# A two-block transformer on one core: loads, panel splits and squares moved to other places in their queues

## The chip, the cores and the metric

The kernel runs on one core of a Trainium2 chip. The metric is device time in microseconds of one execution of the whole program, the median of several runs. Five engines work from instruction queues of their own: TensorE (PE), VectorE (DVE), ScalarE (ACT), GpSimd (POOL) and SyncE (SP), which here issues the large loads. They meet at semaphores.

## The reference

256 tokens of width 1024 go through two models one behind the other, all in float32.

```python
def reference(x, ...):
    x = first_block(x, ...)      # 2 layers: x += hybrid_mixer(rms_norm(x)); x += conv_ffn(rms_norm(x))
    return second_block(x, ...)  # 2 layers: h += 0.5 * rms_norm(swiglu(rms_norm(h)))
                                 #           h += rms_norm(mixer(rms_norm(h)))
                                 #           h += 0.5 * rms_norm(swiglu(rms_norm(h)))
def conv_ffn(h, w_up, conv_w, conv_b, w_down):
    a, g = jnp.split(h @ w_up, 2, axis=-1)
    a = causal_depthwise_conv(a, conv_w) + conv_b          # 3 taps
    return (jax.nn.gelu(a) * g) @ w_down
def swiglu(x, w_gate_up, w_down):
    gate, up = jnp.split(x @ w_gate_up, 2, axis=-1)
    return (jax.nn.silu(gate) * up) @ w_down
```

The hybrid mixer is three kinds of attention with gated branches; the second block's mixers are a short convolution and a gated delta rule (the "delta" stage), whose heads' outputs are normalized: `o * rsqrt(mean(o * o) + eps) * norm_w * silu(z)`, and then multiplied by `w_out`.

## The kernel before

**Stages.** Ten stages in a row: HYBRID, FFN1, HYBRID, FFN1, then FFN2, SHORT, FFN2, FFN2, DELTA, FFN2. Each begins with `turn_x` on TensorE (transposes of x by the identity in `masks`), `prepare` on ACT and `prepare_tile` on DVE, which bring x with its gain into `xhi` and `xlo`, and a root of the row sums. FFN1, FFN2, SHORT and HYBRID then run `blocks_of`, blocks of 128 hidden features: 22 in FFN1 and FFN2, 8 in HYBRID and SHORT. DELTA runs `delta`, 47 slots in an order written out by hand, and then 16 blocks.

**Precision.** Every product of activations and weights is made of three matmuls, hi x hi, lo x hi and hi x lo. A weight panel (128 x 1024, 512 KB) lands in `raw[p % 6]`; ACT copies it into `whi` (`hi(p)`, L988), DVE subtracts and gets `wlo` (`lo(p)`, L1516), and TensorE waits for `lo_done`. The 621 panels form one stream through a ring of six. SP loads panel p once `lo` of panel p-6 is done; `hi(p)` also waits until TensorE has used panel p-6. The stream's order on ACT and DVE is the order in which the code calls `hi_to` and `lo_to`.

**A block** f of an FFN stage: TensorE multiplies two up panels (48 matmuls of 256 columns) and then the down panel of block f-2 (12 matmuls of 512 columns, L2275 to L2277 like the others). DVE scales the up products (`gate_scaled`), ACT applies the tap (L1046) and Gelu (FFN1) or Silu (FFN2), DVE multiplies to h, ACT copies h into `hhi` (L1059), and DVE makes `hlo` from it in block f+1 (`h_low`, L1676). In HYBRID the up product is one panel, and DVE gates three branches (L1617 to L1624). In DELTA's blocks TensorE transposes two tiles of a head's output (L2371) and multiplies the down panel of block f-2; DVE makes h from the transposes (L1667).

**Around the delta stage's end** ACT squares the last set's outputs (`delta_o_squared`, eight squares, L1415) in the last slot, DVE sums them (`delta_o_added`, L2181), ACT takes the root behind block 1, and DVE scales the last two pairs behind block 2.

**The start.** SP issues x, cols, masks and six panels. ACT waits for cols, calls `hi_to(1)` (panels 0 and 1), then `prepare(0)`. DVE calls `lo_to(1)` and then makes the eight `xlo` tiles. TensorE waits for masks and x. GpSimd waits for masks and then issues the small loads of the hybrid stage (w1, w2, pos, gate_w among them, which DVE waits for in tile 1, L1799).

Of the kernel before, what the change touches and what calls it, by code (L numbers as in the profile page):

```python
# [300 lines left out]
def build(nc, stages, arrays):  # L301
# [14 lines left out]
    with ExitStack() as ctx:  # L316
# [459 lines left out]
        def _(sp):  # L776
            sp.dma_start(x[:], x_in).then_inc(x_loaded, 16)
            sp.dma_start(cols[:], cols_in).then_inc(cols_loaded, 16)
            sp.dma_start(masks[:], masks_in).then_inc(masks_loaded, 16)
# [81 lines left out]
        def _(pool):  # L861
# [4 lines left out]
            pool.wait_ge(masks_loaded, 16)  # L866
            def hybrid(s):
# [110 lines left out]
        def _(act):  # L978
# [16 lines left out]
            def prepare(s):  # L995

                for k in range(KT):
                    g, src = turned(s, k)
                    if k == TURNS[g][0]:
                        act.wait_ge(x_turned, len(TURNS) * s + g + 1)  # L1000
                    act.activation(xhi[:, k, :], src, ACT.Copy, scale=col(("pre", s), k)).then_inc(xhi_ready, 1)  # L1001
                if posts_before(s):
                    act.wait_ge(post_squared, QUARTERS * posts_before(s))
# [28 lines left out]
            def ffn_block(s, f, turn):  # L1032
# [7 lines left out]
                elif kind in (FFN2, DELTA):  # L1040
                    act.activation(act_out[:, sl, :], first[:, sl, 2:], ACT.Silu).then_inc(act_done, 1)  # L1041
                elif kind != HYBRID:

                    c = plus(convs_before(s) + f, turn, UNROLL)
                    if kind == FFN1:
                        act.activation(conv[:, sl, :], first[:, sl, 2:], ACT.Identity,  # L1046
                                       scale=tap(s, 2, f, turn), bias=conv_bias(s, f, turn)) \
                            .then_inc(tap_done, 1)
                        act.wait_ge(conv_done, c + 1)
# [9 lines left out]
                act.activation(hhi[:, sl, :], h[:, sl, :], ACT.Copy).then_inc(hhi_done, 1)  # L1059

            def blocks_of(s):
                def body(f, turn):
                    nb = n_blocks(s)
                    if turn is not None:
                        for j in range(n_up(s) + 1):
                            hi(up_panel(s, f + 1, j), turn)
                        split[0] = up_panel(s, nb - 2, n_up(s)) + 1
                    else:
                        hi_to(ahead_panel(s, f + 1 if stages[s][0] == HYBRID and 0 < f < nb - 1 else f))
                    ffn_block(s, f, turn)  # L1070
                    if f == 1 and stages[s][0] == DELTA:
                        delta_o_root(1)
                    if f == nb - 1:
                        hi_to(down_panel(s, f) + LEAD)
                run_blocks(act, s, body)
# [332 lines left out]
            def delta_o_squared(n):  # L1408

                act.wait_ge(d["o_copied"], 2 * (n + 1))  # L1410
                for i in range(SET * CHUNKS):
# [13 lines left out]
            def delta_step(s, n, o):  # L1425
# [17 lines left out]
                if p == 22:  # L1443
                    delta_o_squared(n)
# [40 lines left out]

            act.wait_ge(cols_loaded, 16)
            act.wait_ge(consts_ready, 4)
            hi_to(1)
# [13 lines left out]
        def _(dve):  # L1502
# [95 lines left out]
            def ffn_block(s, f, turn):  # L1598
# [13 lines left out]
                elif kind == HYBRID:  # L1612

                    dve.wait_ge(y["merged"], 3 * KT * (hybrids_before(s) + 1))
# [10 lines left out]
                    if f >= 1:  # L1625
                        h_low(s, f - 1, turn)
# [13 lines left out]
                else:  # L1640
                    dve.tensor_tensor(first[:, sl, 2:], pair[:, 0:S], rstd[:], ALU.mult).then_inc(gate_scaled, 1)  # L1641
                    dve.tensor_tensor(second[:, sl, :], pair[:, S:], rstd[:], ALU.mult).then_inc(pair_read, 1)

# [35 lines left out]
            def blocks_of(s):  # L1679
                def body(f, turn):  # L1680
                    nb = n_blocks(s)
                    if turn is not None:
                        for j in range(n_up(s) + 1):
                            lo(up_panel(s, f + 1, j), turn)
                        split[0] = up_panel(s, nb - 2, n_up(s)) + 1
                    else:
                        lo_to(ahead_panel(s, f))
                    ffn_block(s, f, turn)
                    if f == 2 and stages[s][0] == DELTA:
                        delta_o_inv(1)  # L1690
                        delta_o_scaled((6, 7))
# [510 lines left out]
            def delta_step(s, n, o):  # L2202
# [23 lines left out]
                if p == (23 if n + 1 < SETS else 22):  # L2226
                    delta_o_added(n)
# [29 lines left out]
            dve.wait_ge(consts_ready, 4)  # L2257
            lo_to(1)
            for k in range(KT):
                prepare_tile(0, k)  # L2260
# [11 lines left out]
        def _(pe):  # L2272
# [650 lines left out]
            pe.wait_ge(consts_ready, 4)  # L2923
            pe.wait_ge(masks_loaded, 16)
# [24 lines left out]
```

## Time and profile before

| | |
|---|---|
| runs, median (lowest to highest) | 2023.91 us (2023.28 to 2025.52), 3 runs |
| profiled execution: time, span | 2025.12 us, 2023.3 us |
| TensorE busy (matmuls / weight loads) | 1979.2 us, 98% / 1841.5 us, 91% |
| DVE, ACT, GpSimd busy | 1389.5 us, 69% / 1105.3 us, 55% / 125.4 us, 6% |
| mean granted clock of TensorE | 0.995 |
| mean DMA rate | 172 GB/s |

The span runs from the first to the last instruction of the profiled execution; the time of an execution is a little longer. Busy shares are means over stages with different limits. The granted clock is a share of 2.4 GHz: TensorE runs either at that or at half of it.

### The profile page before, as it was taken

To read this page: it belongs to the slowest core of one execution; us is meant where nothing else is said; L and a number is where in the kernel's file an instruction comes from. 1 tells how busy PE (TensorE), PEld (TensorE's weight loads), DVE (VectorE), ACT (ScalarE), POOL (GpSimd) and SP (SyncE) were. 2 spreads that over 40 slices of the span, in tenths; PEclk is the share of its full clock that TensorE was granted. 3 is DMA by queue.
4 is the path that set the end of the run, shared out by engine and by line. 5 is a ranking of instruction groups with operands and counts; after the bars stand their busy time and mean duration, and the time that the engine had idled before them with its cause. 6 is when DMAs were issued, how large, how long until landed. Compare 5 with 4: busy or idle time off the path is not lost. (4 is left out here: it accounts for less than half of the span.)

```text
span 2023.3 us, 40582 instructions
## 1 busy us (share of the span) xinstructions
PE 1979.2 (98%) x15118; PEld 1841.5 (91%) x15118; DVE 1389.5 (69%) x2352; ACT 1105.3 (55%) x1836; POOL 125.4 (6%) x204
## 2 busy tenths in 40 slices
PE   8999999999999999999999999999999999999998
PEld 6999899989998999899999999999999999979997
DVE  5687877676788777765567765575559876567555
ACT  5665555566654655554454544464448786546443
POOL 2031000000130000000000000000002422000000
PEclk9999999999999999999999999999999999999999
DMA  9433655554335555465546455555555444345552
GB/s 309 146 126 126 210 193 187 191 178 146 133 119 177 178 187 187 167 208 187 188 166 212 154 195 187 187 178 187 188 178 166 134 140 149 126 146 186 187 188 93
DMA packets 117812, 348.42 MB, mean 172 GB/s; under 512 B 23288, under 2 KB 35912, under 8 KB 117184
## 3 DMA queue, kind: packets, MB, share of 16 engines
q1 hardware_dynamic: 114960, 335.23, 48.9%
q0 software_dynamic: 2736, 11.59, 1.8%
q8 instruction: 80, 1.31, 0.3%
q14 instruction: 36, 0.29, 0.0%
HBM read 340.81 MB, written 5.96 MB: 171 GB/s over the span
## 5 line engine op out<-in xcount | busy, mean ns | idle before, releaser
L1516 DVE TENSOR_TENSOR wlo<-raw,whi 128x1024 fp32r<-128x1024 f32 x621 | 737.9, 1229 | 382.6 <-ACT whi L988 381.5
L2275 PE MATMUL bank<-xhi,whi 128*128 128x256 f32 x3368 | 955.5, 284 | 9.7 <-DVE xlo L1527 5.2
L2276 PE MATMUL bank<-xlo,whi 128*128 128x256 f32 x3368 | 941.7, 280 | 0.0
L2277 PE MATMUL bank<-xhi,wlo 128*128 128x256 f32 x3368 | 941.1, 279 | 0.0
L2275 PEld LDWEIGHTS bank<-xhi,whi 128*128 128x128 f32 x3368 | 633.8, 188 | 25.2 <-issue 7.3
L2276 PEld LDWEIGHTS bank<-xlo,whi 128*128 128x128 f32 x3368 | 634.2, 188 | 5.7
L2277 PEld LDWEIGHTS bank<-xhi,wlo 128*128 128x128 f32 x3368 | 633.6, 188 | 0.0
L988 ACT ACTIVATE whi<-raw 128x1024 fp32r<-128x1024 f32 x621 | 621.2, 1047 | 6.8 <-PE bank L2277 5.3
L2275 PE MATMUL bank<-whi,hhi 128*128 128x512 f32 x688 | 273.7, 398 | 6.5 <-DVE hlo L1676 5.1
L2277 PE MATMUL bank<-whi,hlo 128*128 128x512 f32 x688 | 271.6, 395 | 0.0
L2276 PE MATMUL bank<-wlo,hhi 128*128 128x512 f32 x688 | 271.1, 394 | 0.0
L1059 ACT ACTIVATE hhi<-h 128x256 fp32r<-128x256 f32 x172 | 72.1, 419 | 266.7 <-PE bank L2277 182.6
L1041 ACT ACTIVATE act_out<-first 128x256 f32<-128x256 f32 x89 | 37.4, 420 | 230.7 <-DVE first L1641 230.3
L2275 PEld LDWEIGHTS bank<-whi,hhi 128*128 128x128 f32 x688 | 129.5, 188 | 34.8 <-issue 10.5
L2277 PEld LDWEIGHTS bank<-whi,hlo 128*128 128x128 f32 x688 | 129.8, 189 | 30.2
L2276 PEld LDWEIGHTS bank<-wlo,hhi 128*128 128x128 f32 x688 | 130.4, 190 | 23.3
L1641 DVE TENSOR_TENSOR first<-bank,rstd 128x256 f32<-128x256 f32 x132 | 55.8, 422 | 52.8 <-PE bank L2277 52.6
L1676 DVE TENSOR_TENSOR hlo<-h,hhi 128x256 fp32r<-128x256 f32 x172 | 71.8, 417 | 12.6 <-ACT hhi L1059 12.6
L1046 ACT ACTIVATE conv<-first,cols 128x256 f32<-128x256 f32 x44 | 26.5, 603 | 92.9 <-DVE first L1641 92.9
L1670 DVE TENSOR_TENSOR h<-act_out,second 128x256 f32<-128x256 f32 x132 | 55.8, 422 | 22.7 <-ACT act_out L1050 21.6
L1141 ACT ACTIVATE arena<-arena 128x256 f32<-128x256 f32 x48 | 20.0, 418 | 70.2 <-DVE arena L1791 70.2
L929 POOL DMA_DIRECT2D arena<-gains_in x6 | 3.3, 553 | 865.8 <-DVE arena L1555 734.8
(367 smaller groups left out, 1792.6 us busy)
## 6 DMA issues: line engine op xcount, KB each, us to landing
raw<-panels SPq DMA_DIRECT2D x621, 512.0 KB, 4.3
arena<-w_in POOLq DMA_DIRECT2D x2, 2048.0 KB, 10.0
arena<-relay SPq DMA_DIRECT2D x8, 512.0 KB, 4.8
arena<-gains_in POOLq DMA_DIRECT2D x6, 512.0 KB, 4.0
relay<-arena POOLq DMA_DIRECT2D x4, 512.0 KB, 8.1
relay<-arena SPq DMA_DIRECT2D x4, 512.0 KB, 4.1
x<-x_in SPq DMA_DIRECT2D x1, 1024.0 KB, 5.0
arena<-bias_table POOLq DMA_DIRECT2D x8, 128.0 KB, 4.6
```

What stands on the lines that cost most here:

```text
L988: act.activation(whi[slot][:], raw[slot][:], ACT.Copy).then_inc(hi_done, 1)
L1041: act.activation(act_out[:, sl, :], first[:, sl, 2:], ACT.Silu).then_inc(act_done, 1)
L1046: act.activation(conv[:, sl, :], first[:, sl, 2:], ACT.Identity, scale=tap(s, 2, f, turn), bias=conv_bias(s, f, turn)) \
L1059: act.activation(hhi[:, sl, :], h[:, sl, :], ACT.Copy).then_inc(hhi_done, 1)
L1141: act.activation(g, g, ACT.Tanh, scale=0.5).then_inc(y["merged"], 1)
L1516: dve.tensor_tensor(wlo[slot][:], raw[slot][:], whi[slot][:].bitcast(F32), ALU.subtract) \
L1641: dve.tensor_tensor(first[:, sl, 2:], pair[:, 0:S], rstd[:], ALU.mult).then_inc(gate_scaled, 1)
L1670: dve.tensor_tensor(h[:, sl, :], gated, second[:, sl, :], ALU.mult).then_inc(h_done, 1)
L1676: dve.tensor_tensor(hlo[:, sl, :], h[:, sl, :], hhi[:, sl, :].bitcast(F32), ALU.subtract) \
L2275: pe.matmul(dst, w_hi, a_hi, start=start, stop=False, skip_group_check=True)
L2276: pe.matmul(dst, w_hi, a_lo, start=False, stop=False, skip_group_check=True)
L2277: return pe.matmul(dst, w_lo, a_hi, start=False, stop=stop, skip_group_check=True)
```

## The change

In one sentence: the order of work in the queues changes, at the start, in the blocks and around the end of the delta stage; and ten matmuls of ones are added.

- SP: masks are loaded first. GpSimd: it waits for x as well before the small loads.
- ACT: a root of one is the first activation (the table of the roots is loaded at once). `prepare(0)` splits panel 0 ahead of tile 2 of x, and panel 1 behind tile 7. DVE: `lo_to(0)` ahead of tile 2, `lo_to(1)` behind tile 7. TensorE: ten products of ones ahead of its wait for the masks.
- FFN1 and FFN2 on ACT: the panels that were split ahead of block f+1 are split in block f, the first behind Silu or the tap, the others behind `hhi`. On DVE the last low panel ahead of block 0 goes behind the first gate.
- HYBRID on DVE: `h_low(f - 1)` goes ahead of the gating of block f.
- DELTA: ACT splits one down panel further ahead; the last set's squares go behind blocks 1 and 2, their sum and the root behind block 3, and the last scaling behind block 5.

```diff
         def _(sp):
+            sp.dma_start(masks[:], masks_in).then_inc(masks_loaded, 16)
             sp.dma_start(x[:], x_in).then_inc(x_loaded, 16)
             sp.dma_start(cols[:], cols_in).then_inc(cols_loaded, 16)
-            sp.dma_start(masks[:], masks_in).then_inc(masks_loaded, 16)
...
             pool.wait_ge(masks_loaded, 16)
+            pool.wait_ge(x_loaded, 16)
...
                     if k == TURNS[g][0]:
                         act.wait_ge(x_turned, len(TURNS) * s + g + 1)
+                    if s == 0 and k == 2:
+
+                        hi_to(0)
                     act.activation(xhi[:, k, :], src, ACT.Copy, scale=col(("pre", s), k)).then_inc(xhi_ready, 1)
+                hi_to(1)
...
                     act.activation(act_out[:, sl, :], first[:, sl, 2:], ACT.Silu).then_inc(act_done, 1)
+                    for p in ahead[0:1]:
+                        hi(p, turn)
...
                             .then_inc(tap_done, 1)
+                        for p in ahead[0:1]:
+                            hi(p, turn)
                         act.wait_ge(conv_done, c + 1)
...
                 act.activation(hhi[:, sl, :], h[:, sl, :], ACT.Copy).then_inc(hhi_done, 1)
+                for p in ahead[1:]:
+                    hi(p, turn)
...
                     if turn is not None:
-                        for j in range(n_up(s) + 1):
-                            hi(up_panel(s, f + 1, j), turn)
-                        split[0] = up_panel(s, nb - 2, n_up(s)) + 1
+                        ahead = [up_panel(s, f + 2, j) for j in range(n_up(s) + 1)]
+                        split[0] = up_panel(s, nb - 1, n_up(s)) + 1
+                    elif loops(s):
+                        hi_to(ahead_panel(s, f))
+                        ahead = list(range(split[0], ahead_panel(s, f + 1) + 1)) if f < nb - 1 else []
+                        split[0] += len(ahead)
                     else:
-                        hi_to(ahead_panel(s, f + 1 if stages[s][0] == HYBRID and 0 < f < nb - 1 else f))
-                    ffn_block(s, f, turn)
-                    if f == 1 and stages[s][0] == DELTA:
-                        delta_o_root(1)
+                        hi_to(ahead_panel(s, f + 1 if stages[s][0] in (HYBRID, DELTA) and 0 < f < nb - 1 else f))
+                        ahead = []
+                    ffn_block(s, f, turn, ahead)
+                    if stages[s][0] == DELTA:
+                        if f in (1, 2):
+                            delta_o_squared(SETS - 1, range(4 * f - 4, 4 * f))
+                        if f == 3:
+                            delta_o_root(1)
...
-                if p == 22:
-                    delta_o_squared(n)
+                if p == 22 and n + 1 < SETS:
+                    delta_o_squared(n, range(SET * CHUNKS))
...
+            act.wait_ge(consts_ready, 4)
+
+            act.activation(root_of_one[:, 0:1], ones[:, 0:1], ACT.Sqrt)
             act.wait_ge(cols_loaded, 16)
-            act.wait_ge(consts_ready, 4)
-            hi_to(1)
             prepare(0)
...
                 elif kind == HYBRID:
 
+                    if f >= 1:
+                        h_low(s, f - 1, turn)
                     dve.wait_ge(y["merged"], 3 * KT * (hybrids_before(s) + 1))
...
                     dve.tensor_tensor(h[:, sl, :], second[:, sl, :], conv[:, sl, :], ALU.add).then_inc(h_done, 1)
-                    if f >= 1:
-                        h_low(s, f - 1, turn)
                     return
...
                     dve.tensor_tensor(second[:, sl, :], pair[:, S:], rstd[:], ALU.mult).then_inc(pair_read, 1)
+                    if f == 0:
+                        lo_to(ahead_panel(s, f))
...
+                    elif loops(s) and f == 0:
+
+                        lo_to(ahead_panel(s, f) - 1)
                     else:
                         lo_to(ahead_panel(s, f))
                     ffn_block(s, f, turn)
-                    if f == 2 and stages[s][0] == DELTA:
+                    if f == 3 and stages[s][0] == DELTA:
+                        delta_o_added(SETS - 1)
+                    if f == 5 and stages[s][0] == DELTA:
                         delta_o_inv(1)
                         delta_o_scaled((6, 7))
...
-                if p == (23 if n + 1 < SETS else 22):
+                if p == 23 and n + 1 < SETS:
                     delta_o_added(n)
...
             dve.wait_ge(consts_ready, 4)
+            for k in range(KT):
+                if k == 2:
+                    lo_to(0)
+                prepare_tile(0, k)
             lo_to(1)
-            for k in range(KT):
-                prepare_tile(0, k)
             prepare_rstd(0)
...
             pe.wait_ge(consts_ready, 4)
+            for i in range(10):
+
+                pe.matmul(bank[2][:, 0:P], ones[:], ones[:], start=True, stop=True)
             pe.wait_ge(masks_loaded, 16)
```

## Rows read from the trace of the kernel before

**Rows 1.** Waits of all TensorE instructions: line, releaser, us in total, times, longest.

```profile
PE bank L2275 <- DVE hlo L1676: 5.1, 7, 1.7
...
PE bank L2275 <- DVE wlo L1516: 2.3, 3, 1.0
```

**Rows 2.** Timeline of the start: start, us, engine, line, operation, count, idle before.

```profile
6.97 3.65 PE L2318 MATMUL bank<-masks,x 128*128 128x128 f32 x16 [6.97 <-DMA masks<-masks_in]
...
8.27 1.28 ACT L988 ACT_TABLE_LOAD   x1 [8.27 <-DMA raw<-panels]
...
10.75 2.36 DVE L1516 TENSOR_TENSOR wlo<-raw,whi 128x1024 fp32r<-128x1024 f32 x2 [10.75 <-ACT whi L988]
11.47 3.01 ACT L1001 ACTIVATE xhi<-bank,cols 128x256 fp32r<-128x256 f32 x8
...
13.03 3.22 DVE L1527 SCALAR_TENSOR_TENSOR xlo<-bank,cols,xhi 128x256 fp32r<-128x256 f32 x8
...
13.66 0.36 PE L2275 MATMUL bank<-xhi,whi 128*128 128x256 f32 x1 [3.04 <-DVE xlo L1527]
...
16.78 1.28 ACT L1011 ACT_TABLE_LOAD   x1
...
21.25 0.48 PE L2275 MATMUL bank<-whi,xhi 128*128 128x512 f32 x1
...
24.64 0.65 DVE L1799 COPY arena<-tmp 128x240 f32<-128x240 f32 x2 [0.67 <-DMA arena<-gate_w_in]
```

**Rows 3.** DMA issues of the first 40 us: KB each, us from issue to landing.

```profile
x<-x_in SPq DMA_DIRECT2D x1, 1024.0 KB, 5.0
```

**Rows 4.** Timeline, first blocks of the first hybrid stage, DVE and TensorE.

```profile
201.94 1.23 DVE L1516 TENSOR_TENSOR wlo<-raw,whi 128x1024 fp32r<-128x1024 f32 x1 [1.44 <-ACT whi L988]
...
204.88 0.42 DVE L1676 TENSOR_TENSOR hlo<-h,hhi 128x256 fp32r<-128x256 f32 x1
...
205.44 0.47 PE L2275 MATMUL bank<-whi,hhi 128*128 128x512 f32 x1 [1.71 <-DVE hlo L1676]
```

**Rows 5.** Timeline, blocks 2 and 3 of the first FFN1 stage, DVE and TensorE.

```profile
264.23 3.50 DVE L1516 TENSOR_TENSOR wlo<-raw,whi 128x1024 fp32r<-128x1024 f32 x3 [1.43 <-ACT whi L988]
...
265.60 0.36 PE L2275 MATMUL bank<-xhi,whi 128*128 128x256 f32 x1 [1.03 <-DVE wlo L1516]
```

**Rows 6.** Timeline, first blocks behind the delta slots, DVE and TensorE.

```profile
1765.17 0.24 DVE L2181 SCALAR_TENSOR_TENSOR arena<-arena 128x4 f32<-128x4 f32 x2 [2.83 <-ACT psq L1415]
...
1767.08 0.41 PE L2371 MATMUL bank<-masks,arena 128*128 128x128 f32 x2 [1.96 <-DVE h L1667]
```

**Rows 7.** Timeline, one later block behind the delta slots, and the last wait there.

```profile
1776.90 1.05 ACT L988 ACTIVATE whi<-raw 128x1024 fp32r<-128x1024 f32 x1
...
1777.98 1.23 DVE L1516 TENSOR_TENSOR wlo<-raw,whi 128x1024 fp32r<-128x1024 f32 x1 [1.44 <-ACT whi L988]
...
1779.17 0.38 PE L2371 MATMUL bank<-masks,arena 128*128 128x128 f32 x2
...
1779.68 0.47 PE L2275 MATMUL bank<-whi,hhi 128*128 128x512 f32 x1
1779.97 0.42 ACT L1059 ACTIVATE hhi<-h 128x256 fp32r<-128x256 f32 x1 [2.02 <-DVE h L1667]
1780.29 1.04 ACT L988 ACTIVATE whi<-raw 128x1024 fp32r<-128x1024 f32 x1
...
1817.31 0.47 PE L2275 MATMUL bank<-whi,hhi 128*128 128x512 f32 x1 [0.69 <-DVE hlo L1676]
```

**Rows 8.** Windows of TensorE: us, busy (instructions), granted clock, DMA share, GB/s.

```profile
14.00:17.50 3.50, 3.50 (x20) 0.54 1.08 439
...
21.00:25.00 4.00, 4.00 (x20) 1.00 0.99 383
...
1767.90:1772.40 4.50, 4.41 (x12) 0.62 0.29 107
```

**Rows 9.** Panel loads of the first FFN1 stage, landing times.

```profile
DMA to landing us min/median/max: 3.1/4.5/5.2
```

More of the change, by code:

```diff
@@ L1030, in finish, with ffn_block @@
                 hi_to(down_panel(s, n_blocks(s) - 1) + LEAD + 1)
-            def ffn_block(s, f, turn):
+            def ffn_block(s, f, turn, ahead):
                 kind, sl = stages[s][0], f % 2
@@ L1406, in delta_o_copied, with delta_o_squared @@
                     act.activation(o_pair(KSET * n + g), bank[g][:], ACT.Copy).then_inc(d["o_copied"], 1)
-            def delta_o_squared(n):
+            def delta_o_squared(n, parts):
                 act.wait_ge(d["o_copied"], 2 * (n + 1))
-                for i in range(SET * CHUNKS):
+                for i in parts:
                     at = SET * CHUNKS * n + i
```

## The prediction

> **What bounds the kernel now.** I read the page first, then the list of waits of TensorE, then the timeline of all engines around each wait, and the windows for the clock. TensorE is busy for 98% of the span, so nothing is to be had inside its steady stretches: the change can only give back time in which TensorE stands still, or runs at the low clock. Its listed waits are 33 and sum to 33.4 us. In [rows 1] the reader is to see that the waits for the low halves (of h, and of the panels, both written by DVE from what ACT split) are few and long: they sit at the edges of stages, not in every block. The timeline places them:
>
> - Start [rows 2]. The first transposes wait for the masks until 6.97. ACT does nothing before 8.27, when panel 0 has landed, loads a table, splits panels 0 and 1, and only then x. DVE makes both low panels first, to 13.0, then xlo; the first product comes at 13.66. The stretch from 14 to 17.5 runs at 0.54 of the clock, so mostly at the low level, 1.2 GHz [rows 8]: TensorE had stood still for 3 us before it. The root of the norm waits for a second table load at 16.78, the splits of panels 2 and on follow it, and panel 2 starts on TensorE at 21.25.
> - Hybrid stages [rows 4]. hlo of block 0 is made at 204.88, behind the gating of block 1, and TensorE waits 1.71; the second hybrid stage shows the same at 623.90.
> - FFN1 stages [rows 5]. The low panel that block 3 wants is started at 264.23, since DVE itself waited 1.43 for ACT's split; TensorE waits 1.03; the same at 684.10.
> - End of the delta stage [rows 6]. DVE's sums at 1765.17 waited 2.83 for eight squares on ACT, the first h stands behind them, and TensorE waits 1.96. Its first down product then takes 4.41 us for 12 matmuls at 0.62 of the clock [rows 8].
> - The blocks after it [rows 7] list almost no idle time, and this is what the list of waits hides. A block takes 3.39 us, and so does a loop of ACT and DVE: split of a panel 1776.90, its low half 1777.98 and behind it hlo and h, hhi at 1779.97 when h is there, next split 1780.29. TensorE transposes at 1779.17 and starts its product at 1779.68, right behind hlo. By itself a block would be the product's 2.88 (3.39 less the 0.51 ahead of it) and two transposes at full clock, 0.1 each (half of the first stage's 0.228): 3.08.
>
> **The change part by part.**
> *Start.* Masks go first on SP; x is issued 0.45 later with 192 KB more ahead of it. Before, x took 5.0 from an issue at 0.8 [rows 3], so the transposes move to some 6.4 from 6.97. That decides little, since panel 0 still lands near 8.3 (the same bytes are ahead of it). By then ACT has its table and two tiles of x (0.375 each, 3.01 / 8). Panel 0 is split from 8.4 to 9.45, DVE's low half is there at 10.65, the first product at 10.8. ACT splits six more tiles to 11.7 and panel 1 to 12.75. DVE makes six xlo (0.40 each, 3.22 / 8) to 13.05 and the low half of panel 1 to 14.25. So TensorE runs panel 0 from 10.8 to 13.4 and panel 1 from 14.35 to 17.1. The two squares end at 15.35, the root, with no table load, at 15.65; panel 2 is split at 16.65, its low half done at 17.9. Panel 2 starts at 18.0 for 21.25: 3.25 less.
> Against it: DVE has to pass its wait for the small loads, which ended at 24.6 [rows 2], before it makes the low half of panel 5. That wait is 0.67; with all else three microseconds earlier it is about 3.5, panel 5 is ready at 26.5 and wanted near 27. The reserve is half a microsecond, and the small loads now compete with panel loads that are issued earlier. I take off 0.25 (bounds 0 and 1.5): 3.0 for the start.
> The ten products of ones lie in the time before x. At the 0.228 of the first transposes (3.65 / 16, half speed by the matmuls of the same size later) they take 2.3 us, from 1.1 to 3.4, with 3 us to spare; past 6.4 each would cost its whole length. I price them at nothing, bounds 0 and 0, and take the clock as full from 10.8 on since TensorE no longer stands still for 3 us before panel 0. If a low stretch like that of [rows 8] stays, it costs half of its 3.2 us, 1.6. GpSimd's added wait for x (6.4 against the 6.97 of the masks before) delays nothing: behind it stand only the small loads.
> The Trainium skill (ScalarE: Activation LUTs, section "What ACT_TABLE_LOAD costs") counts 1.28 us for a load and 1.38 for a drain on top. The row shows the 1.28 alone, and the root's load starts right behind the squares. By the page the start would gain 1.4 more.
>
> *Hybrid.* hlo goes ahead of the gating. It can start when the low panel is made, 201.94 + 1.15 = 203.1, and is there at 203.5. TensorE, free near 203.6, starts there for 205.44: 1.8 for each of two stages, 3.6. The gating slips by one operation, 0.33. What waits for gating is the h of two blocks on; the wait for hhi that now stands ahead of it ends before the branch products do in the later blocks, so it is free there.
>
> *FFN1 and FFN2.* ACT splits the first panel of block f+2 behind the first activation of block f, the others behind hhi; DVE's last low panel before block 0 goes behind the first gate. So the tap of block 0 comes one low panel, 1.1, earlier. The split of the panel that block 3 wants moves from behind hhi to behind the tap of block 1, and DVE, which stood idle from 262.8 [rows 5], gets to it 1.1 earlier, at 261.7: done at 262.9, wanted at 265.60 - 1.03 = 264.6. The wait goes, twice: 2.1. In steady blocks TensorE keeps its own pace, and ACT's split falls into the time in which it waits for DVE's taps or h: worth nothing. Without that cover a split costs 1.05, and still has most of a block before TensorE wants its hlo.
>
> *Delta stage.* The squares go behind blocks 1 and 2, the root behind 3, the last scaling behind 5 (TensorE wants it at block 12), and ACT splits one down panel ahead. DVE then has its low panel at 1763.5, h at 1763.95, ACT hhi at 1764.4, DVE hlo at 1764.9. TensorE ends its last z product at 1765.0, and at full clock is done with the first down product at 1768.05 for 1772.4 [rows 8]: 4.35. The loop loses its split. What is left on DVE is low panel, hlo and h, 2.0 (1777.98 to 1779.97), and on ACT 1.5, so TensorE sets the pace: 12 spacings at 3.08 for 3.39 are 3.7. At the end the wait of 0.69 at 1817.31 goes, and with it I estimate 0.55 of restarts in the last three products, which come behind a stop today: 1.25. Together 9.3. Bounds: 5.5 where the spacing stays, 10.5 with a block at 3.0.
>
> **Sum.** 3.0 + 3.6 + 2.1 + 9.3 = 18.0. The profiled execution took 2025.12 (its span 2023.3); less 18.0 is 2007.1. The median of the runs shown is 1.2 under it, so I forecast 2005.9.
>
> **The rivals.**
> 1. A block at the end of delta is TensorE's own 3.39. For it: almost no idle time is listed there. Against: the product starts right behind hlo in each, and 0.5 between the transposes and the product is twice what two of them need at full clock. Then 3.8 and some of the rest are missing: 2010.2. Chance 0.12.
> 2. The start's gain is lost to the loads. The DMA engines are full until 25 us (0.99 in [rows 8]), the small loads end at 24.6 whatever TensorE does, and the panel loads issued earlier push them out; with a low stretch of the clock too, 2.5 of the 3.0 go: 2008.4. Chance 0.18. A rule of the Trainium skill stands beside it (DMA: Bandwidth & Descriptors, "Issuing engines are not separate DMA queues"): what SP and GpSimd issue runs on the same 16 engines and interleaves. The late landing of the small loads agrees.
> 3. Slower: ACT works in order, and splits now stand ahead of the Gelu and of h's copy. If a panel has not landed, that holds up h in all of some 110 looping blocks. A slot's load is issued when its low panel is made, which is over one block, by my estimate 11 us, before the new place of its use; landings take 4.5, at most 5.2 [rows 9]. Once a landing passes the slack of TensorE, each 0.2 us in a block makes 22 us: 2028. Chance 0.02.
> 4. The change does not do what it says at the two hidden places: only the start and the first block after delta move, 3.0 + 4.35: 2016.6. Chance 0.05.
> 5. The forecast: 0.63.
>
> The long wait for the relay near 1583 and the low clock after it aren't touched; where such a stretch falls can shift the time by 1.7 either way. It is in the range.
>
> **Numbers.** A measurement of this kernel can tell 0.2%, 4 us, from no change. The likeliest case has 2003.5 to 2008.5. Cases 1 and 2 with the shift of the clock reach to 2012; cases 3 and 4, 0.07, are left out, and some of both tails. So 2003 to 2012. Faster by over 0.2% wants less than 2019.9: 0.96. Same 0.02, slower 0.02.
>
> **What would show it.** The first product near 10.8, panel 2 near 18.0; one table load in ACT's first 20 us; no wait of TensorE for hlo in the hybrid stages, none for a low panel at block 3 of FFN1; in the delta stage 0.2 to 0.3 between transposes and product, a spacing near 3.1, no low clock at its end. I am wrong if the spacing stays at 3.39, if DVE's wait for the small loads passes on to TensorE by over 1 us, or if ACT newly waits for panel loads in the FFN stages.

## The result and the profile after

The changed kernel takes 2002.53 us (median of 4 executions, 1999.64 to 2004.08); the kernel before, run beside it, 2024.59 (2023.28 to 2025.52). The ratio is 0.989, 95% interval 0.9873 to 0.9907: 22.1 us faster, where 18.0 were forecast. The time lies 0.5 under the low end of the range. The profiled execution took 2003.59, its span is 2000.6; before they were 2025.12 and 2023.3, so the spans differ by 22.7 and the profiled times by 21.5.

TensorE's waits after the change, the five largest (columns as in [rows 1]). There is no line for hlo, where 5.1 us stood, and the waits for low panels are 1.9:

```profile
PE bank L2782 <- DMA arena<-relay: 3.7, 1, 3.7
PE bank L2303 <- DVE xlo L1546: 2.2, 5, 0.4
PE bank L2337 <- DVE sq L1581: 2.1, 5, 0.4
PE bank L2303 <- DVE arena L2029: 2.1, 3, 1.0
PE bank L2303 <- DVE wlo L1535: 1.9, 4, 0.7
```

The start after the change, in the timeline, against [rows 2]:

```profile
1.13 4.63 PE L2954 MATMUL bank<-ones 128*128 128x128 f32 x20 [1.13 <-POOL eps_col L865]
6.60 3.65 PE L2346 MATMUL bank<-masks,x 128*128 128x128 f32 x16 [0.84 <-DMA x<-x_in]
...
8.58 1.06 ACT L989 ACTIVATE whi<-raw 128x1024 fp32r<-128x1024 f32 x1 [0.38 <-PE bank L2346]
...
10.95 0.39 PE L2303 MATMUL bank<-xhi,whi 128*128 128x256 f32 x1 [0.70 <-DVE wlo L1535]
...
14.86 0.19 ACT L1013 ACTIVATION_READ_ACCUMULATOR psq<-x 128x1 f32 x1
15.08 0.30 ACT L1016 ACTIVATE row_root<-row_sums,eps_col 128x2 f32<-128x2 f32 x1
...
17.71 0.48 PE L2303 MATMUL bank<-whi,xhi 128*128 128x512 f32 x1
...
25.84 0.67 DVE L1825 COPY arena<-tmp 128x240 f32<-128x240 f32 x2 [4.02 <-DMA arena<-gate_w_in]
26.50 1.23 DVE L1535 TENSOR_TENSOR wlo<-raw,whi 128x1024 fp32r<-128x1024 f32 x1
27.78 0.50 PE L2303 MATMUL bank<-whi,xhi 128*128 128x512 f32 x1 [0.50 <-DVE wlo L1535]
```

Panel 0 is split at 8.58, the first product is at 10.95 and panel 2 at 17.71 (forecast 8.4, 10.8 and 18.0). The root follows the squares with no load between. DVE's wait for the small loads grew from 0.67 to 4.02 and passes 0.50 on to TensorE.

The first blocks behind the delta slots, against [rows 6] and [rows 7]:

```profile
1752.84 0.39 PE L2399 MATMUL bank<-masks,arena 128*128 128x128 f32 x2
1752.98 0.48 PE L2303 MATMUL bank<-whi,hhi 128*128 128x512 f32 x1
...
1755.85 0.38 PE L2399 MATMUL bank<-masks,arena 128*128 128x128 f32 x2
...
1758.85 0.38 PE L2399 MATMUL bank<-masks,arena 128*128 128x128 f32 x2
1758.98 0.48 PE L2303 MATMUL bank<-whi,hhi 128*128 128x512 f32 x1
...
1759.11 0.42 ACT L1068 ACTIVATE hhi<-h 128x256 fp32r<-128x256 f32 x1 [0.46 <-PE bank L2305]
```

TensorE waits for nothing here. From the start of the transposes to the start of the product it is 0.13 us in place of 0.51, and 3.00 from block to block in place of 3.39. ACT's copy into hhi now waits for TensorE to be done with the buffer: TensorE sets the pace.

**Where the time came from.** Each stage's norm begins with a few spread products (bank from masks and rstd_tok, L2353). The table takes them as marks. Each number is in us and says how much TensorE gained in that part on the trace of the kernel before; a row is one trace, named by what was edited. The relay column goes from the norm at 1528.34 to the transposes at 1761.71, the last but one from there to the norm at 1834.99.

| trace | start + hybrid 1 | FFN1 | hybrid 2 | FFN1 | FFN2, short | relay | end of delta | all |
|---|---|---|---|---|---|---|---|---|
| forecast | 4.8 | 1.05 | 1.8 | 1.05 | 0 | 0 | 9.3 | 18.0 |
| changed | 4.46 | 2.99 | 1.69 | 2.86 | 0.09 | 0.01 | 10.66 | 22.76 |
| changed, again | 4.63 | 3.06 | 1.65 | 2.87 | 0.04 | 0.76 | 10.50 | 23.51 |
| no ahead in loop stages | 4.63 | 0.81 | 1.69 | 0.80 | 0.05 | 2.43 | 10.50 | 20.91 |
| ahead in blocks 0-2 only | 4.14 | 3.03 | 1.64 | 2.88 | 0.13 | 2.12 | 10.53 | 24.47 |
| low panels before the gate | 4.76 | 2.99 | 1.68 | 2.88 | -0.01 | 1.19 | 10.50 | 23.99 |
| late splits in delta | 4.64 | 3.02 | 1.70 | 2.96 | 0.10 | 0.24 | 0.78 | 13.44 |
| squares back in the slot | 4.47 | 3.06 | 1.64 | 2.88 | 0.06 | 2.44 | 6.23 | 20.78 |
| no ones | 3.79 | 3.03 | 1.73 | 2.97 | -0.05 | 1.71 | 10.53 | 23.71 |
| 12 ones in relay wait | 4.58 | 2.88 | 1.69 | 3.04 | 0.07 | 0.80 | 10.53 | 23.59 |
| low half 5 ahead | 4.57 | 3.03 | 1.65 | 3.01 | -0.01 | 2.76 | 10.50 | 25.51 |
| both, 4 ones | 5.62 | 3.03 | 1.62 | 3.00 | 0.14 | 2.09 | 10.50 | 26.00 |
| before, another trace | 0.55 | 0.12 | 0.02 | 0.10 | 0.10 | 1.44 | 0.02 | 2.35 |

All columns but the relay's repeat to 0.1 or 0.2 from trace to trace where nothing that bears on them was edited (the start to 0.6). Two terms are off: FFN1, 5.85 for 2.1, and the end of delta, 10.66 for 9.3.

### The profile page after: what moved, and what is told of

The parts are those of the page before. It is cut to its first block, busy times and chain, and to the rows that moved or that the text cites. A ratio compares the mean times of both kernels' runs of the same rounds, so it can differ in the third digit from the quotient of the medians.

```text
span 2000.6 us, 40608 instructions
## 1 busy us (share of the span) xinstructions
PE 1977.1 (99%) x15138; PEld 1844.8 (92%) x15138; DVE 1401.8 (70%) x2352; ACT 1099.0 (55%) x1836; POOL 124.2 (6%) x204
## 4 chain that ended last, share of the span: by engine, by line
PE 91%; DVE 3%; DMA 2%; ACT 2%; POOL 1%; issue 1%; DVEq 0%; SPq 0%; ACTq 0%; POOLq 0%
PE bank L2303 28%; PE bank L2305 27%; PE bank L2304 27%; PE bank L2782 2%; PE bank L2593 1%; DVE arena L1574 1%; ACT whi L989 1%; DMA arena<-gate_w_in 1%; DVE wlo L1535 1%; PE bank L2337 1%; PE bank L2566 0%; POOL arena L972 0%; PE bank L2554 0%; PE bank L2346 0%; DMA arena<-relay 0%
## 5 line engine op out<-in xcount | busy, mean ns | idle before, releaser
L1535 DVE TENSOR_TENSOR wlo<-raw,whi 128x1024 fp32r<-128x1024 f32 x621 | 750.3, 1231 | 208.0 <-ACT whi L989 205.0
L989 ACT ACTIVATE whi<-raw 128x1024 fp32r<-128x1024 f32 x621 | 632.3, 1045 | 11.3 <-PE bank L2305 5.6
```

Of the source, the lines that this page charges most:

```text
L989: act.activation(whi[slot][:], raw[slot][:], ACT.Copy).then_inc(hi_done, 1)
L1535: dve.tensor_tensor(wlo[slot][:], raw[slot][:], whi[slot][:].bitcast(F32), ALU.subtract) \
```

## Experiments on the FFN1 stages

**No splitting ahead in the looping stages.** In the loop ACT splits the panels of block f+1 at the block's front again, and DVE's deferred low panels stand where they stood:

```diff
-                        ahead = [up_panel(s, f + 2, j) for j in range(n_up(s) + 1)]
+                        for j in range(n_up(s) + 1):
+                            hi(up_panel(s, f + 1, j), turn)
...
-                    elif loops(s):
-                        hi_to(ahead_panel(s, f))
-                        ahead = ...
...
-                    if f == 0:
-                        lo_to(ahead_panel(s, f))
```

> The changed kernel, with ACT's splits in the FFN1 and FFN2 blocks put back ahead of the block (one edit undone). Theory A (the 3.0 us that each FFN1 stage gives come from ACT's earlier splits, 1.4 at its first blocks and 1.55 at its end, where the last gate no longer stands behind two late low panels): both waits come back, TensorE waits about 1.0 in block 3 and about 1.0 for DVE's update of x at the end of each FFN1 stage, 5.5 to 6 us in all, time near 2008.3. Rival B (the stage's start gains by DVE's low panel behind the first gate alone): only the end comes back, 3.1 us, 2005.6. Rival C (neither edit matters to the end, which moved by the phase of the blocks): under 1 us.

2005.54 (2004.3 to 2006.78), ratio 0.9904 (0.9888 to 0.9921). The stages give 0.81 and 0.80. Two waits are back in each, at the start and at the end, in the timeline of TensorE:

```profile
260.29 0.36 PE L2301 MATMUL bank<-xhi,whi 128*128 128x256 f32 x1 [0.51 <-DVE wlo L1533]
426.84 2.26 PE L2344 MATMUL bank<-masks,x 128*128 128x128 f32 x16 [1.05 <-DVE x L1596]
```

So ACT's earlier splits are worth 2.18 and 2.07 us. That is theory A in kind, since both waits are back, but smaller: 4.25 in the two stages for 5.5 to 6. (The medians differ by only 3.0, rival B's size. The trace is 2.4 ahead in the relay column, so the time alone can't tell the two apart.) A good part of it lies at the stage's end, which I had not priced, though the list of TensorE's waits in the kernel before has a line for it, two waits of 1.0 (at 432.25 and 850.75):

```profile
PE bank L2318 <- DVE x L1579: 2.1, 2, 1.0
```

What it is, the groups of DVE from 300 to 400 us show, in the middle of the stage, where TensorE waits for nothing. Before:

```profile
L1641 DVE TENSOR_TENSOR first<-bank,rstd 128x256 f32<-128x256 f32 x12 | 5.0, 418 | 0.0
```

After:

```profile
L1660 DVE TENSOR_TENSOR first<-bank,rstd 128x256 f32<-128x256 f32 x12 | 5.1, 425 | 13.6 <-PE bank L2305 13.6
```

This is the gate, the first thing that DVE does with a block's products. After the change it stands waiting for TensorE, 1.13 in each of 12 blocks. Before, it never waited: DVE was behind in every block. From the start of the down product that TensorE multiplies in a block to that block's gate it is 6.04 us in block 2 of before, 3.82 in block 5, 3.31 in block 20 and 1.75 in the last; after, 0.20 from block 5 on. The loop of ACT and DVE was nearly as long as TensorE's block: its gates come 8.30 and 8.41 apart in turn, 8.355 in the mean, and those of the changed kernel 8.39 and 8.38. So a lag of 3.6 more than after, taken on in the first blocks, shrank by some 0.03 a block, hidden from TensorE. In the last block, whose gate comes 6.83 behind the one before it, DVE makes up 1.56. What is left, 1.75 against 0.20, is the 1.55 that the stage gives at its end, where x has to be whole. The end of the stage, before:

```profile
424.01 0.42 DVE L1641 TENSOR_TENSOR first<-bank,rstd 128x256 f32<-128x256 f32 x1
...
430.83 2.48 DVE L1579 TENSOR_TENSOR x<-x,bank 128x512 f32<-128x512 f32 x4
...
432.25 2.26 PE L2318 MATMUL bank<-masks,x 128*128 128x128 f32 x16 [1.04 <-DVE x L1579]
```

and after:

```profile
416.56 0.42 DVE L1660 TENSOR_TENSOR first<-bank,rstd 128x256 f32<-128x256 f32 x1 [2.60 <-PE bank L2305]
...
423.38 2.47 DVE L1598 TENSOR_TENSOR x<-x,bank 128x512 f32<-128x512 f32 x4
...
424.81 2.26 PE L2346 MATMUL bank<-masks,x 128*128 128x128 f32 x16
```

**Ahead in blocks 0 to 2 alone.** Is it the lag, or the order in the last two blocks, that makes x late?

```diff
-                        ahead = [up_panel(s, f + 2, j) for j in range(n_up(s) + 1)]
+                        ahead = []
+                        for j in range(n_up(s) + 1):
+                            hi(up_panel(s, f + 1, j), turn)
...
-                        ahead = list(range(...)) if f < nb - 1 else []
+                        ahead = list(range(...)) if f < 3 else []
```

> The changed kernel, but in FFN1 and FFN2 ACT splits a block ahead only in blocks 0, 1 and 2; from block 3 on its order is that of the kernel before. Theory A (a lag from the stage's start is carried through the whole stage, because ACT and DVE's loop is hardly quicker than TensorE's, and it is what makes x late at the end): with the lag gone by block 3, most of the end's wait of 1.04 us stays away, TensorE waits under 0.5 us before the transposes behind FFN1, and the lead that an FFN1 stage adds is 2.3 to 2.9 us. Rival B (the end's own order counts: in the last two blocks the splits stand ahead of the tap): the wait of about 1.04 us is back in both FFN1 stages, each adds 1.4 to 1.9 us, and the time is 2 to 2.5 us above the changed kernel's.

2001.19 (2000.02 to 2001.63), ratio 0.9881 (0.9865 to 0.9898). The stages give 3.03 and 2.88, and TensorE waits neither in block 3 nor for x at the end: theory A. The same group of DVE, 300 to 400 us:

```profile
L1662 DVE TENSOR_TENSOR first<-bank,rstd 128x256 f32<-128x256 f32 x12 | 5.0, 418 | 0.0
```

Steady blocks have the order and the pace of before, and DVE is behind in each of them here too. But the lag is 1.66 us in block 5 and 1.10 in block 20, where before it was 3.82 and 3.31, and the last block makes up the rest: its gate comes 0.20 behind, as in the changed kernel. What counts is how much lag the first blocks leave, not how the others are ordered.

**DVE's low panels before the gate again**, the added lines of block 0 taken out:

```diff
-                    if f == 0:
-                        lo_to(ahead_panel(s, f))
...
-                    elif loops(s) and f == 0:
-                        lo_to(ahead_panel(s, f) - 1)
```

> The changed kernel, with DVE's last low panel put back ahead of block 0's gate in FFN1 and FFN2. Theory A (both edits are needed for block 3 of FFN1): the tap of block 0 is 1.1 later and part of the wait in block 3 comes back, at most 1.4 in each of two stages; 0 to 2.8 us slower. Rival B (ACT's earlier splits alone remove the wait): no difference within 0.5 us in the place of TensorE's rows.

2001.71 (2000.96 to 2002.8), ratio 0.9885 (0.9868 to 0.9901), 2.99 and 2.88: nothing is lost, rival B. My argument for the 2.1 ran over DVE getting to block 0's tap a low panel earlier; ACT's splits do it alone.

**The kernel before with its last two blocks split early.**

```diff
                     else:
+                        if f == nb - 2 and loops(s):
+                            hi_to(ahead_panel(s, f + 1))
```

> The kernel before with a single edit: in FFN1 and FFN2 ACT splits the last two down panels behind block 20 in place of ahead of block 21. Theory A (the FFN1 stage's end loses its stop by this alone): TensorE's wait of 1.04 for x at the end of both FFN1 stages goes, 1.55 each, 3.1 us faster than before, 2021.5. Rival B (it takes the lead of all blocks, carried from the stage's start): no difference.

2024.57 (2022.76 to 2026.39, 10 executions), ratio 0.9997 (0.9987 to 1.0007). It tells nothing of either theory: the edit was ill made, since panels split behind block nb-2 come ahead of block nb-1 in either kernel, and ACT's order is that of before. What it leaves is a second trace of the kernel before, the last row of the table: outside the relay column it is 0.9 us ahead, 0.55 of it from the start.

## Experiments on the end of the delta stage

**Splits late again, squares still moved:**

```diff
-   hi_to(ahead_panel(s, f + 1 if stages[s][0] in (HYBRID, DELTA) and 0 < f < nb - 1 else f))
+   hi_to(ahead_panel(s, f + 1 if stages[s][0] == HYBRID and 0 < f < nb - 1 else f))
```

> The changed kernel, with ACT's one-panel lead in the delta blocks undone; the squares stay moved. Theory A (a loop of ACT and DVE with the split in it sets 3.39 per block): the spacing of the transposes goes back to 3.39, TensorE's product again starts 0.5 behind them, 12 spacings by 0.39 and the end's stop: 5 to 6 us slower than the changed kernel, near 2008. Rival B (3.39 against 3.00 comes from the squares, the sum and the last scaling, which stood in ACT's and DVE's queues): the spacing stays at 3.00, no difference.

2012.22 (2011.03 to 2013.15), ratio 0.9935 (0.9919 to 0.9952): of 10.66, 0.78 is left. Rival B is refuted. Theory A has the cause, but the loss, 9.7 us by the time, is well over the 5 to 6 that it expected. TensorE waits in the blocks that now carry the squares and the root, and at the end:

```profile
1756.81 0.47 PE L2303 MATMUL bank<-whi,hhi 128*128 128x512 f32 x1 [1.12 <-DVE hlo L1697]
...
1761.38 0.47 PE L2303 MATMUL bank<-whi,hhi 128*128 128x512 f32 x1 [1.32 <-DVE hlo L1697]
...
1766.29 0.47 PE L2303 MATMUL bank<-whi,hhi 128*128 128x512 f32 x1 [1.66 <-DVE hlo L1697]
...
1803.88 0.47 PE L2303 MATMUL bank<-whi,hhi 128*128 128x512 f32 x1 [0.69 <-DVE hlo L1697]
```

By the third transposes (1755.31, for 1772.40) TensorE has won 4.43 us since the slots, as in the changed kernel. Then three blocks take 4.37, 4.57 and 4.89 for 3.39, which gives 3.66 back, and the rest keep 3.39.

**Squares back between the o passes, splits early:**

```diff
-                if p == 22 and n + 1 < SETS:
+                if p == 22:
                     delta_o_squared(n, range(SET * CHUNKS))
...
-                        if f in (1, 2):
-                            delta_o_squared(SETS - 1, range(4 * f - 4, 4 * f))
...
-                    if f == 3 and stages[s][0] == DELTA:
-                        delta_o_added(SETS - 1)
```

> The changed kernel with the last eight squares back between the o passes, and the sum with them; the root stays behind block 3 and the scaling behind block 5, and ACT splits down panels one ahead. Theory A (the long wait and low clock at the first down product is the squares' doing, the spacing the splits'): TensorE waits some 2 us again near 1755, its first down product runs at the low clock for part of its length, 3 to 4.4 us of the 10.7 are lost, and the spacing of the later blocks stays at 3.0: 2005.5 to 2007. Rival B (the split one panel ahead carries nearly all, as the run with late splits suggests): under 1.5 us is lost, 2002.5 to 2004.

2005.35 (2004.33 to 2007.83), ratio 0.9907 (0.989 to 0.9923); 6.23 at the end of delta, 4.3 less: theory A. TensorE in the timeline:

```profile
1752.53 0.41 PE L2395 MATMUL bank<-masks,arena 128*128 128x128 f32 x2 [1.96 <-DVE h L1686]
1753.43 0.74 PE L2299 MATMUL bank<-whi,hhi 128*128 128x512 f32 x1 [0.50 <-DVE hlo L1695]
...
1757.86 0.38 PE L2395 MATMUL bank<-masks,arena 128*128 128x128 f32 x2
...
1760.86 0.38 PE L2395 MATMUL bank<-masks,arena 128*128 128x128 f32 x2
```

The wait of 1.96 of [rows 6] and the 0.50 behind it are back, the first down product takes 4.43 us from there as before, and the spacing stays at 3.00. The two halves of the edit do not add up: moving the squares gives 0.8 by itself and 4.3 on top of the splits, since only the slack that the early splits make can carry eight squares and a root.

## Experiments on the clock, the start and the relay

**Without the ten products of ones.**

```diff
-            for i in range(10):
-                pe.matmul(bank[2][:, 0:P], ones[:], ones[:], start=True, stop=True)
```

> The changed kernel without the ten products of ones. Theory A (they are hidden and what keeps the clock up later is that TensorE stands still for less than before): no change, the first product at 10.9 to 11.0 and full clock from there, lead at the first norm within 0.4 us of the changed kernel's. Rival B (they warm the clock): the transposes run as before, but part of the products behind 10.95 runs at the low clock, as 14 to 17.5 did before; 1 to 2 us later at the first norm, 2003.5 to 2004.5.

2002.42 (2001.42 to 2003.82), ratio 0.989 (0.9874 to 0.9907). Its products from 10.76 to 15.6 stand 0.213 us apart, those of the changed kernel 0.117, and the window from 12 to 14 us holds 11 of them. (Its columns: us; busy time and count of TensorE's matmuls, of its weight loads, of DVE, ACT and GpSimd; granted clock; DMA share; GB/s.)

```profile
12.00:14.00 2.00, 2.00 (x11) 2.00 (x11) 2.00 (x4) 1.91 (x4) 1.23 (x3) 1.00 1.03 409
```

The changed kernel has 18 there:

```profile
12.00:14.00 2.00, 2.00 (x18) 1.81 (x16) 2.00 (x5) 1.91 (x4) 1.53 (x4) 1.00 1.03 384
```

So theory B as to the pace: TensorE keeps half its pace until 15.8 here, and in the changed kernel, where the ones stand ahead of the transposes, it has the full one from 10.95. The 1.00 in both rows is no contradiction. The trace's record of the clock begins at 15.78 here and at 10.77 in the changed kernel, each time with the full clock, and a window ahead of it shows 1.00 because nothing is recorded. In all thirteen traces the matmuls ahead of the first record stand at the half pace (0.213 from one to the next, as where the record says 0.50) and those behind it at the full one, so TensorE was at 1.2 GHz until then. The first norm comes 1.4 us later than in the changed kernel. At the next norm only 0.67 of it is left, because the wait at 27.78 is not there when TensorE comes later; in the time it is within the scatter. This is one trace without the ones.

**Low half of panel 5 ahead of the wait for the small loads:**

```diff
                     if t == 1:
+                        if n == 0:
+                            lo_to(p0 + 5)
                         dve.wait_ge(y["small_loaded"], 64 * (n + 1))
```

> The changed kernel, but DVE makes the low half of panel 5 ahead of its wait for the small loads in the first hybrid stage. Theory A (of the start's lead 0.5 to 0.9 is given back at 27.8 because that wait stands ahead of the low half): the wait of TensorE at 27.78 goes, the lead behind the first hybrid stage grows from 4.46 to 4.9 to 5.4, and the time falls by 0.5 to 0.9. Rival B (TensorE soon waits for the next low half or for the small loads' users instead, since the panels land late): under 0.2 us is left of it at the end of the stage.

1999.96 (1998.65 to 2003.55), ratio 0.9877 (0.9861 to 0.9894). The time is lower by more than the edit can account for (the relay column of its trace is the highest, 2.76). In its trace the start tells nothing, since a low stretch of the clock fell into it (first norm at 17.93) and hid the wait in any order. The same edit in the run with both edits, below, with the first norm at 16.89, gives 5.62 behind hybrid 1 against 4.63 in the changed kernel's second trace (first norm at 16.82, wait 0.79 at 27.56): 1.0 us, and the wait is gone: theory A, which had priced it at 0.5 to 0.9.

**Twelve products of ones in the relay wait:**

```diff
-                pe.wait_ge(d["tri_in"], 16 * (n + 1))
                 pe.wait_ge(d["v_copied"], 2 * (n + 1))
+                if n == 0:
+                    for i in range(12):
+                        pe.matmul(bank[0][:, 0:P], ones[:], ones[:], start=True, stop=True)
+                pe.wait_ge(d["tri_in"], 16 * (n + 1))
```

> The changed kernel with twelve products of ones put into TensorE's long wait for the relay (3.67 us at 1571.88), ahead of that wait. Theory A (the clock falls behind the wait because TensorE stood still): the twelve take up to 5.5 us at the low clock or 2.8 at the full one, the wait shrinks by as much, the stretch from 1572 to 1581, at 0.50 in the changed kernel, runs at 0.8 or more, and the time falls by 1 to 4 us, to 1998.5 to 2001.5. Rival B (the clock falls there for another reason, or the small products don't count): the low stretch stays where it is, no gain, or up to 1.5 us lost where the twelve outlast the wait.

2001.79, the median of four executions of 2000.1, 2001.53, 2002.05 and 7977.12 (the last unexplained); ratio 0.9882 (0.9862 to 0.9901), which leaves the last out. The twelve run from 1570.17 to 1574.4 and outlast the relay, whose products start 2.5 us later than in the changed kernel. The low stretch is shorter (windows with the columns given above):

```profile
1572.00:1576.00 4.00, 4.00 (x26) 4.00 (x25) 3.53 (x8) 2.32 (x5) 0.00 (x0) 0.66 1.05 349
1576.00:1580.00 4.00, 4.00 (x38) 4.00 (x37) 2.43 (x4) 1.23 (x2) 0.00 (x0) 1.00 0.69 235
```

In the changed kernel the clock is 0.50, the level of 1.2 GHz, in both windows:

```profile
1572.00:1576.00 4.00, 4.00 (x20) 4.00 (x20) 3.93 (x10) 2.32 (x5) 0.00 (x0) 0.50 1.07 373
1576.00:1580.00 4.00, 4.00 (x20) 4.00 (x21) 1.31 (x3) 1.39 (x2) 0.00 (x0) 0.50 0.67 221
```

The relay column is 0.80, inside what traces without these products show. So there is no gain, as rival B has it, and the shorter stretch can't be laid to the twelve: five changed traces without them have one as short.

**Both, with four products** (the edit of panel 5, and range(4) for range(12)); "the version before" in the text is the kernel with the edit of panel 5:

> The version before with four products of ones in TensorE's wait for the relay, instead of the twelve that outlasted it by 2.5 us. They fit: 0.9 to 1.9 us in the 1.7 us between the values' copy and the relay's landing. Theory A (TensorE's standing still is what brings the low stretch on, so that the shortened stop leaves less of it): the products at 1572 run at the full clock, and 0.5 to 3 us are gained on the version without. Rival B (the low stretch comes whatever fills the last part of the wait): the granted clock is again 0.5 to 0.6 from 1572 on, and the time is that of the version without, to within the scatter around the relay.

1999.76 (1999.36 to 2000.3), ratio 0.9873 (0.9856 to 0.9889), the fastest here. But of the gain over the changed kernel only the 1.0 at the start can be laid to an edit. The low stretch is 3.4 us long, as in the run with the edit of panel 5 alone; the relay column has 2.09 for 2.76 there, and the times are the same to 0.2. The four products gained nothing: rival B as to the time.

**The changed kernel again:**

> The changed kernel, nothing edited, for the size of its own scatter beside the two versions that follow. Both theories expect the leads of its first trace (3.5 to 4.0 at the first norm, 12.1 to 12.4 behind the second FFN1 stage, 10.4 to 10.7 more behind the delta stage's blocks) except around the relay wait near 1572. Theory A (what happens there, a low stretch of the clock and a second wait near 1697, is scatter): the lead there moves by up to 2.7 us from trace to trace and the time is 2000.5 to 2003.5. Rival B (it belongs to the order of each kernel): the lead there falls by 1.2 again and comes back at 1711, as in the first trace.

2002.53 (2000.89 to 2004.53), ratio 0.9888 (0.9871 to 0.9904). The relay column is 0.76 for 0.01, with nothing edited: one kernel scatters there. Over the eleven traces with changed code the column runs from 0.01 to 2.76, and in the second trace with the order of before it is 1.44.

Two things make up most of that column. One is the low stretch of the clock at the first relay wait, which the trace records with its length:

| low stretch | traces | gained from the norm at 1528.34 to the end of the stretch |
|---|---|---|
| 10.2 us | changed; late splits | -1.23, -1.19 |
| 6.8 | before (the zero); changed, again; low panels | 0, -0.46, -0.26 |
| 3.4 | before, another; no ahead; blocks 0-2; squares back; no ones; low half 5 | 1.29 to 1.50 |
| 3.4, ones in the wait | 12 ones; both, 4 ones | 0.28, 1.43 |

The longer the stretch, the more is lost. What sets its length stays open; it differs between two traces of one kernel.

The other is a second relay wait, at 1710.88 in the trace of before, 1.20 long. Both traces with the order of before have it (1.20 and 1.26). It is gone in ten of the eleven changed traces, which gain 1.2 to 1.4 us there, and 0.85 is left in the one without the ones. So some 1.2 us may belong to the change and not to scatter, at a place that the prediction does not name. In the changed kernel's first trace the long low stretch hid it (-1.23, then +1.22). No run tests which edit removes it. (Three traces, blocks 0-2, 12 ones and both with 4 ones, lose 0.7 between the two places.)

## Why the prediction came out as it did

The direction was right, and so were the places that the prediction named. The time was missed low, by one place that it did not name and by two sizes.

- **Start**, forecast 3.0, measured 2.77. Panel 2 came at 17.71 (forecast 18.0). The lead at the first norm is 3.54, of which 0.77 went back by the route named, the small loads. The root follows the squares (last read 14.86, root 15.08), as its load did before: only the 1.28 of the load went. The Trainium skill (ScalarE: Activation LUTs, "What ACT_TABLE_LOAD costs") would add a drain of 1.38. No row here shows one, and here the measurement decides. The small loads landed at 25.84 for 24.64, with SP's first reload of a panel slot issued at 11.07 for 12.16. This agrees with the rule of the Trainium skill that what SP and GpSimd issue shares the engines (DMA: Bandwidth & Descriptors, "Issuing engines are not separate DMA queues"). The 0.77 is a third of the 2.5 that rival 2 would have taken.
- **The ones**, forecast 2.3 us long and worth nothing: the prediction took the clock as full from 10.8 on because TensorE no longer stood still for 3 us. The number held, the reason did not. Without the ones TensorE stands still for only 0.70 ahead of its first product and still keeps half its pace until 15.8, which costs 1.4 at the first norm and 0.7 behind hybrid 1. They took 4.63 and not 2.3, at 0.23 for each of 20 records, since every product is two; they still ended before x came at 6.60.
- **Hybrid**, forecast 3.6, measured 1.69 and 1.69.
- **FFN1**, forecast 2.1, measured 5.85. This is the step that failed: "The wait goes, twice: 2.1." It prices the edit by the one wait in block 3 and puts the end of the stage at nothing, without a reason. The first stage gave 1.44 by the end of that wait (lead 4.46 at the norm, 5.90 behind block 3) and 1.55 at its end, because DVE's lag from the first blocks is handed on to where x has to be whole; the second gave 2.86 in all. The runs with and without early splits show it: 3.03 and 2.88 with them in blocks 0 to 2 alone, 0.81 and 0.80 with none. The sentence behind, that splits in steady blocks are "worth nothing", holds: left as before from block 3 on they cost nothing.
- **Delta**, forecast 9.3, measured 10.66. First blocks 4.44 for 4.35. The mis-sized term is the 12 spacings: 3.00 and not 3.08, so 4.67 for 3.7. I had put two whole transposes, 0.2, ahead of each product, and it starts 0.13 behind their start. Tail 1.32 for 1.25, and 0.2 behind. The 0.55 of restarts in it was an estimate that no run shows by itself. Rival 1 (a block is TensorE's own 3.39) is refuted.
- **Rival 3** (splits hold up Gelu and h) did not come: TensorE waits for no h and no panel in the FFN stages, and ACT's three waits for panel loads, 5.4 us in all, end by 26.65, in the first hybrid stage. Rival 4 is refuted by both hidden gains.

The terms: 18.0 - 0.2 (start) - 0.2 (hybrid) + 3.75 (FFN1) + 1.36 (delta) + 0.1 is 22.8, the table's total. The 0.1 has luck in it: at the relay the first trace lost 1.2 and gained 1.2. The profiled times differ by 21.5, the medians by 22.1. Without the 3.75 of FFN1 the time would have been in the range.

## What to carry to other kernels

A wait list of the bound engine shows where a lag ends, not where it is made. Ask of the helper engine whether its first operation on a block ever waits for the bound engine. If its idle time there is 0.0, it is behind in every block. That alone is no price: here a lag of 1.1 us in the last block but one cost nothing, and one of 3.3 cost 1.55, since the last block can make up 1.56. So measure the lag ahead of the next point where all has to be whole. What exceeds the slack there is what an edit in the first blocks can win. Work can be moved into a loop only where that loop has slack, so price such a move together with the edit that makes the slack. And compare a small gain by marks stage by stage: one stretch alone scattered here by 2.7 us.

## What I had not expected of the hardware

- The granted clock of a window reads 1.00 where the trace has no record of the clock, and at the start it has none: TensorE ran at half its pace to 15.78 without the ones (0.213 between products) under a 1.00. The count of instructions in a window shows the pace, and the first record stands where the pace doubles.
- The 16 records of the first transposes took 3.65 in three of the traces of changed kernels and 1.94 to 2.16 in the other eight, where the first record stands earlier (4.21 to 6.77). Eight of these traces have a stop of 2.03 to 2.34 us ahead of the first product. In two of them (stops of 2.24 and 2.32) the clock fell to 0.50 behind it, from 11.45 to 14.86 and from 11.04 to 14.45; in the other six it did not.
- Each fp32 product of a 128x128 by 128x128 is two records, 0.46 us at the half pace; a transpose of the same size is one.
